# One SyncE queue, six weight buffers: loading 32 experts' weights in another order

## The reference, cut to what matters

```python
logits = h @ w_router + b_router
top_logit, top_idx = lax.top_k(logits, 4)
gates = softmax(top_logit)
# for each expert e, for the tokens that chose it:
g = minimum(xb @ w_gate[e] + b_gate[e], 7)
u = clip(xb @ w_up[e] + b_up[e], -7, 7)
act = g * sigmoid(1.702 * g) * (u + 1)
y   = act @ w_down[e] + b_down[e]      # weighted by the gate, added to the token's row
```

## Time and profile before

| | us |
|---|---|
| median of 3 runs (lowest, highest) | 2595.76 (2593.84, 2597.33) |
| the profiled execution's own time | 2592.33 |
| its span in the profile | 2590.6 |
| PE busy in the span | 2471.4 (95%) |
| experts: item 0's first matmul to the last scatter | 214.1 to 1184.5 |

### The profile page before, as it was taken

One profiled execution on the slowest core, in us unless ns is written; L12 is line 12 of the kernel. 1 busy time (PEld: TensorE's weight loads), 2 busy tenths in 40 slices (PEclk: granted clock), 3 DMA queues, 4 the chain that ended last, 5 costly groups with the idle time before them and its releaser, 6 DMA issues. The chain is left out here.

```text
span 2590.6 us, 34225 instructions
## 1 busy us (share of the span) xinstructions
PE 2471.4 (95%) x13181; PEld 1544.5 (60%) x13182; DVE 1162.9 (45%) x2368; ACT 373.3 (14%) x759; POOL 45.6 (2%) x65
## 2 busy tenths in 40 slices
PE   7999999999999999998999999999999999999998
PEld 3653333333333333336888868777886995676984
DVE  2732221112211121114484258746996656454566
ACT  2222111111111111111113110011001100132000
POOL 0000000000000000000000000000110000000000
PEclk9999999999999999999999999999999999999999
DMA  9547999999998899997634369754997653314551
GB/s 366 223 174 276 427 427 429 427 428 428 428 427 333 346 428 428 427 427 274 227 130 163 130 232 344 274 183 152 361 380 264 228 162 130 137 66 153 164 193 50
DMA packets 191134, 728.36 MB, mean 281 GB/s; under 512 B 9808, under 2 KB 103342, under 8 KB 163286
## 3 DMA queue, kind: packets, MB, share of 16 engines
q1 hardware_dynamic: 171432, 651.31, 64.5%
q0 software_dynamic: 19632, 76.09, 7.4%
HBM read 726.31 MB, written 1.05 MB: 281 GB/s over the span
## 5 line engine op out<-in xcount | busy, mean ns | idle before, releaser
L1642 PE MATMUL bank<-first_raw,experts_xs 128*64 128x512 f32 x2112 | 485.9, 608 | 49.3 <-DMA first_raw<-in_w_gate 42.8
L1642 PEld LDWEIGHTS bank<-first_raw,experts_xs 128*64 128x64 f32 x2112 | 150.0, 139 | 353.1 <-issue 284.1
L1795 DVE COPY tiled_spread<-bank 128x256 f32<-128x256 f32 x33 | 14.0, 424 | 707.4 <-PE bank L1675 707.4
L1642 PE MATMUL bank<-first_raw,tiled_act_s 128*64 128x512 f32 x1056 | 237.8, 592 | 1.4 <-DVE tiled_act_s L1834 1.4
L1960 PE MATMUL bank<-hT,ring 128*128 128x256 f32 x1024 | 223.4, 380 | 1.4 <-ACT hT L437 1.4
L1960 PEld LDWEIGHTS bank<-hT,ring 128*128 128x128 f32 x1024 | 194.6, 191 | 30.1 <-issue 3.8
L2432 PEld LDWEIGHTS bank<-hT,big 128*128 128x128 f32 x1408 | 162.1, 192 | 11.6 <-issue 11.6
L1642 PEld LDWEIGHTS bank<-first_raw,tiled_act_s 128*64 128x64 f32 x1056 | 76.9, 137 | 151.1 <-issue 151.1
L2432 PE MATMUL bank<-hT,big 128*128 128x128 f32 x1408 | 164.7, 275 | 2.1 <-DVE hT L477 2.1
L2557 PE MATMUL bank<-big,ffn_actT 128*128 128x512 f32 x352 | 154.7, 592 | 0.0
L319 DVE SCALAR_TENSOR_TENSOR layer_sums<-ring,cact,layer_sums 128x512 f32 (+1 forms) x210 | 140.5, 747 | 0.7 <-DMA ring<-in_mod_w 0.7
(11 more groups left out here) (511 smaller groups left out, 2876.3 us busy)
## 6 DMA issues: line engine op xcount, KB each, us to landing
first_raw<-in_w_gate SPq DMA_DIRECT2D x64, 2048.0 KB, 13.9
first_raw<-in_w_up SPq DMA_DIRECT2D x64, 2048.0 KB, 19.2
first_raw<-in_w_down SPq DMA_DIRECT2D x64, 2048.0 KB, 10.5
big<-in_ffn_w_gu SPq DMA_DIRECT2D x88, 1024.0 KB, 7.7
ring<-in_mod_w POOLq DMA_DIRECT2D x30, 2048.0 KB, 10.7
big<-in_ffn_w_down SPq DMA_DIRECT2D x44, 1024.0 KB, 5.1
ring<-in_w_in SPq DMA_DIRECT2D x16, 2048.0 KB, 8.3
first_raw<-in_w_mod SPq DMA_DIRECT2D x19, 1024.0 KB, 5.9
```

Of the source, the lines that this page charges most:

```text
L1642: last = nc.tensor.matmul(bank[b][h * HALF:(h + 1) * HALF, :], stationary(kt), raw[p][:, k, h * C:(h + 1) * C], start=kt == 0, stop=kt == ...
L1795: vec.tensor_copy(spread[:], bank[X][:, 0:SEQ]).then_inc(spread_ready, 1)
```

## The change

The SyncE program of the stage issues the same 186 loads of 2 MB in another order. Expert 1's gate goes ahead of the loop; in a turn of the loop for expert e come U of e, and then the gate of e+1 and the down of e in alternating halves; U and D of expert 31 follow behind the loop. Each load waits for the same semaphore value as before. TensorE, ScalarE and VectorE have the same instructions in the same order.

```diff
-    def load(self, sp, which, m, free=None):
+    def load(self, sp, which, m, free=None, halves=(0, 1)):
         which = which if not isinstance(which, int) else slice(which, which + 1)
-        for q in range(self.parts):
+        for q in halves:
             p = self.parts * m + q
             if free is not None:
                 free(p)
...
-            def load(e, m):
-                last = ended(e - 1)
+            def load(e, last, m, halves=range(PARTS)):
                 which = slice(e, e + 1) if isinstance(e, int) else bass.ds(e, 1)
-                weights.load(sp, which, m, lambda p: sp.wait_ge(used[p], last))
-
-
-            with sp.Fori(1, E) as e:
-                for m in range(3):
-                    load(e, m)
+                weights.load(sp, which, m, lambda p: sp.wait_ge(used[p], last), halves)
+
+            load(1, ended(0), 0)
+            with sp.Fori(1, E - 1) as e:
+                last, ends = ended(e - 1), ended(e)
+                load(e, last, 1)
+                for q in range(PARTS):
+                    load(e + 1, ends, 0, [q])
+                    load(e, last, 2, [q])
+            last = ended(E - 2)
+            for m in (1, 2):
+                load(E - 1, last, m)
             core.first_w_in_2(sp)
```

## The result

| | before | changed |
|---|---|---|
| median of 5 runs, us | 2595.76 | 2608.21 |
| lowest and highest, us | 2593.84, 2597.33 | 2603.68, 2610.11 |
| profiled execution's own time, us | 2592.33 | 2603.68 |
| its span, us | 2590.6 | 2602.0 |

The ratio is 1.005 with a 95% interval of 1.0039 to 1.006: the change made the kernel 12.4 us slower by the medians. The forecast was 2607, +11.0. The profiled execution was the fastest of the five runs of the changed kernel, 4.5 us under their median; that of before lay 3.4 us under its median.

The account below looks back on a forecast made before the run. TensorE and the loads were taken to be within 0.8 us a turn of each other. The terms -12.0 + 25.8 + 3.4 - 6.2 = +11.0 us, put on the median 2595.8, gave 2607 us, range 2601 to 2618.

Parts of the forecast that it names:

- turn 2 to the start of turn 21: Ordinary turns: each load goes out when its buffer is free, so turn 21 begins 12.0 us earlier.
- the two waits in turn 21: Expert 20's second item: each down half is held behind a gate half of expert 21, 12.9 us each, 25.8 us lost.
- slow matmuls behind them: Lower TensorE clock after each wait in turn 21: 2 x 1.7 = 3.4 us lost, high end 6.8, low end 0.
- turns 22 to 32: Turns after the stalls: nothing is late, so they run at 28.60 us each and 6.2 us come back.
- turn 32's start to the last down product: The tail: the last down weights are there as before, 29.2 us apart, nothing gained or lost.
- the rival with 2614.5: Slow matmuls stay in all six turns, coming with a turn's lightness and not with waits: +7.7 us; chance 0.12.
- The rival of the short stall: Turn 21: the pair is not served in order, Da20 lands 7.8 us after issue; +0.8, about 2597 us; chance 0.08.
- The one with -18.2: Turn 21: no stall if Ga21's wait were content with item 20's use alone; two gains stand, 2577.6 us; chance 0.06.

Follow-up runs that it names:

- the branch: Changed kernel with SyncE branching on expert e's item count: one item alternates gate and down halves, more issues both down halves first; 2576.63 us.
- the kernel with one more second item: Changed kernel with one more item for expert 10, which adds nothing to the result, so two experts have two items; 2666.09 us.
- the two reordered ones: Changed kernel with each down half ahead of the gate half, 2594.97 us; changed kernel with the second gate half behind both down halves, 2601.4 us.
- The old order without a second item: Kernel before with items per expert cut to one, leaving out tokens beyond 64 of expert 20, 32 items in place of 33; 2570.1 us.
- The two queues: Kernel before with gate loads of experts 1 to 31 issued by GpSimd in its own loop, only up and down by SyncE; 2586.06 us.

## Why the prediction was right

Term by term, in the two profiled executions:

| step of the prediction | forecast, us | measured, us |
|---|---|---|
| turn 2 to the start of turn 21 | -12.0 | -11.2 |
| the two waits in turn 21 | +25.8 | +25.9 |
| slow matmuls behind them | +3.4 | +3.5 |
| turns 22 to 32 | -6.2 | -6.3 |
| turn 32's start to the last down product | 0 | 0.0 |
| not forecast: ahead of turn 2 | 0 | -2.2 |
| not forecast: from the last down product to the next block | 0 | +1.2 |

**Ordinary turns, right.** Turn 2's tick less 10.57 is 264.67; turn 21 begins 546.6 behind it, forecast 545.9, before 557.8. The 0.7 us lies in turns 17 to 20, where late loads cost some 3.3 us and not 2.5. The loads were to be late from about turn 17 on; the first long tick is turn 18's. The slow first halves of the earlier trace rows are gone outside turn 21, as the forecast had it; the rival with 2614.5 is refuted by turns 2 to 16 and 22 to 32, which all tick at 28.6.

**Turn 21, right.** 58.42 us against 28.60 is 29.8 more: 25.9 of waiting, 5.83 - 3.65 = 2.2 and 5.00 - 3.65 = 1.35 of lower clock, 0.4 left over. That the slow matmuls add up to the forecast's 3.4 is in part luck: one is above the 1.7 taken for each and one below. Behind the four such waits of the kernel with one more second item they cost 1.6, 2.7, 1.45 and 2.6, so a pair cost 3.5 to 4.3 in all that were seen. The rival of the short stall, with the down half landing after 7.8 us, is refuted: it took 12.3 from its own issue. The one with -18.2 was right in its two gains, which is why the branch brings 17.0, and wrong in its condition.

**The rest.** The 2.2 us ahead of turn 2 and the 1.2 behind the last down product are differences between executions. In the profiled execution of before the first gate half of turn 1 was slow (6.13 us); in that of the changed kernel it was not (3.65). From item 0's tick to turn 1's it is 24.3 us in five of the ten profiled executions of this document, 26.0 in three and 27.7 in two. From the last down product to the next block's first product it is 23.4 us in two of them (the kernel before and the one with the down half ahead) and 24.2 to 25.0 in the others. The old order is found in the short and in the long group each time, so neither is a price of the new one. In the profiled pair they are 1.0 us in favour of the changed kernel, which is why the pair differs by 11.4 and the medians by 12.4; that the forecast of 11.0 meets the pair's number so closely is in part this. The changed kernel's other four runs, whose granted clock was 0.989 to 0.991 against the profiled one's 0.992, are 3.4 to 6.4 us slower than it. Where those microseconds lie is open; each of those runs left only its clock and its span.

The measured column adds up to 10.9, and with the 0.4 left over in turn 21 to 11.3; the spans differ by 11.4.

**What is shown and what argued.** That the loss hangs on the second item, grows with the number of such experts and goes with the order of two queue entries is shown by seven runs: two without a second item, two with two, the two reordered ones and the branch. That the 17 us won by the branch are the earlier loads and the regained slow matmuls is shown by the ticks of two orders, not by a run that separates the two.

## What to carry to other kernels

An in-order queue is a promise about the order in which waits end. Before reordering loads to match the common case, look for the case in which a consumer comes round again, here an expert with a second item, and ask of each load what stands ahead of it and who releases that; a load that the releaser itself needs next must not stand behind. When the order depends on data, branch on the data in the queue that issues the loads: a waiting queue has time for it. And where a loop's engine and its loads are within 3% of each other, write the buffer's release times and the landings side by side with the unwaited period: the crossing point can be worked out to a turn or a few.

## What the runs showed of the hardware

TensorE's granted clock fell at some of the waits for loads that stand at a turn's start. Each of those turns' starts follows a light stretch: transposes, a short wait for VectorE, and then the idle time, of which 0.8 us is the late load's. Busy time of PE (first number after the length, with its count), PEld, DVE, ACT, POOL, then the clock, of two stretches in the kernel before:

```profile
380.00:382.00 2.00, 1.33 (x8) 0.27 (x4) 1.90 (x4) 0.85 (x2) 0.00 (x0) 1.00 1.00 426
382.00:384.00 2.00, 0.65 (x4) 0.34 (x6) 0.81 (x6) 0.00 (x0) 0.00 (x0) 1.00 1.06 451
```

The old order without a second item waits there for the gate's load in 29 turns (235 to 1200 us: total, times, longest):

```profile
PE bank L1643 <- DMA first_raw<-in_w_gate: 46.4, 29, 2.0
```

These counts say which semaphore came last, not that a load was late: in the kernel before, TensorE was idle for longer than 1.3 us at 14 of the 27 starts, and in this kernel at 15 of the 29. The rest are the 1.2 us that stand there anyway. This kernel has seven intervals of 31.1 us between ticks, as this one of turns 5 and 6:

```profile
362.78 0.60 ACT L1752 ACTIVATE tiled_g_rows<-bank 128x512 f32<-128x512 f32 x1 [13.06 <-PE bank L1643]
393.91 0.60 ACT L1752 ACTIVATE tiled_g_rows<-bank 128x512 f32<-128x512 f32 x1 [14.78 <-PE bank L1643]
```

The order with down ahead waits 15 times for the second gate half, in the middle of the products:

```profile
PE bank L1647 <- DMA first_raw<-in_w_gate: 9.0, 15, 0.7
```

The two queues wait 14 times for the second up half, at most 0.7 us too. Neither has such an interval. The rows, then: at the turns' starts all six slow first halves of the kernel before and all seven of the old order without a second item follow an idle time of 1.96 to 2.04 us, and thirteen fast ones follow one of the same length (compare turns 5 and 6 in the earlier trace rows). Turn 1's slow first half in the kernel before follows no wait at all. Behind the 1.2 us of a load that isn't late there is no slow one. Each slow first half of turns 2 to 32 costs 1.7 us. In mid-turn, waits of up to 0.7 us left the clock alone, and the waits of 6.1 to 13.1 us were all followed by slow matmuls, 1.35 to 2.7 us for each. Whether the small waits in mid-turn are harmless for where they stand or for being shorter is not shown.

The prediction took the price of the first kind, 1.7 us, for the second. In the sum that made a difference of 0.1 us in this execution.
